# DeltaNet's inverse: the transposed copy made by transposing T, a new order of ScalarE's work between its levels, and the last heads' fillers in half units

## The chip, the cores and the metric

One core of a Trainium2 chip runs the whole program. The metric is the device time of one launch in microseconds (us), the median of the runs; a second number, the profiled execution, has its own time. TensorE is called PE in the profile, VectorE DVE, ScalarE ACT, GpSimd POOL, SyncE SP.

## The reference, cut to what matters

A trunk of two layers on 512 tokens of width 1024: gated DeltaNet, then differential attention, each followed by a gated convolutional FFN, all in float32. In DeltaNet each of 8 heads projects gate, q, k and v, convolves them over time, and solves a unit lower triangular system per chunk:

```python
low = jnp.where(strict, jnp.einsum('nbhid,nbhjd->nbhij', kb, k) * decay, 0.0)
a_mat = low + jnp.eye(C, dtype=f32)
rhs = jnp.concatenate([v * beta[..., None], kb * jnp.exp(gc)[..., None]], -1)
sol = lax.linalg.triangular_solve(a_mat, rhs, left_side=True, lower=True, unit_diagonal=True)
...
o = rms_norm(o, norm_w) * jax.nn.silu(gate.reshape(B, T, GDN_HEADS, GDN_DV))
return o.reshape(B, T, GDN_V) @ w_out
```

## The kernel before, in words

**Engines and order.** Each engine runs its own program, written out by hand in a fixed order; semaphores with counted values (`d_pe`, `d_dve`, `d_act`, `lo_ready`, `hi_ready`, ...) tie them. An instruction that waits holds all that stands behind it on its engine.

**Products in two halves.** A large product a*b is taken as three matmuls of 512 columns, a_hi*b_hi, a_hi*b_lo and a_lo*b_hi, all in fp32r. Each chunk of 128x1024 weights is loaded by SP into one of two `raw` buffers, rounded by ScalarE into `w_hi` (`split_hi`, L342), and VectorE makes the remainder `w_lo` (`split_lo`, L347); SP may load chunk c when the lo half of chunk c-2 is done, and PE may use a chunk when its lo half is done. The last four chunks of an output weight go to buffers of their own (`hold_hi`, `hold_lo`), which come free when DeltaNet's own tiles are done.

**A head's step.** While PE works head h of DeltaNet it fills the time between dependent small matmuls with pieces of the projections of head h+1: 32 pieces (`fill(p, p+1)` is one piece of three matmuls, L1533 to L1535), four chunks of eight pieces (gate, q, k, v). Small matmuls in plain float32 are two records each, transpositions one record each; `four` (L1588, or L1586 for a transposition) does all four chunks of 128 tokens.

**The inverse.** T (tile `TM`) starts as the inverse of the diagonal 8x8 blocks and doubles its blocks in four levels, s = 8, 16, 32, 64. T's transpose (`TT`) is carried beside it. One level is: P = LT*T by PE (`four`, L1588); a mask on it by VectorE into `PB` (L1084); fillers; `part(1, TT, PB, s, 0)` and `part(2, PB, TT, s, 1)` (L1595, 64 columns for each chunk of tokens), the update of T and that of TT; VectorE adds the first into `TM` (L1094, not at level 64) and the second into `TT` (L1097). Only the very first TT, before level 8, comes from a transposition, copied by ScalarE (L719). After the last level the head's V, W and the state are worked in a chain over the four chunks (L1657 to L1676), then a mean square (L1685), whose root and gate are applied by VectorE (o1, og, hi, lo; L1176 to L1182) into `u_hi`, `u_lo`.

**ScalarE between the levels:** copy of TT; silu of q and q's square for head h+1; the weight halves 8 and 9; the convolution's first tap for k; half 10.

**Last heads.** Head 7 has no next head to project: its fillers are units of the output projection (`mixer_unit(0, tb, k)`: token block tb, head k, two halves of three matmuls, L1521 to L1523), tb 0 and 1 for k = 0 to 6. They begin with a wait for both banks 0 and 1 to be read. The differences of the decay rows (L685) are the first thing that ScalarE does in a step. After the step four units of tb 2 stand before the wait for head 7's result. In attention the last head has units of its output projection as fillers in the same way, by the list `ATT_FILL`; chunks 2h+3 and 2h+4 of its q and k weights are split in step h.

Of the kernel before, what the change touches and what calls it, by code (L numbers as in the profile page):

```python
# [63 lines left out]
GDN_AHEAD = HEADS - 1  # L64
ATT_AHEAD = HEADS - 2
ATT_FILL = [(1, 0, 0), (7, 0, 1), (8, 0, 2), (9, 0, 3), (10, 1, 0), (11, 1, 1), (12, 1, 2), (13, 1, 3), (14, 0, 4),
            (14, 1, 4), (15, 0, 5), (15, 1, 5)]
# [33 lines left out]
def levels(first, then=()):  # L101
    return [f"P{LEVELS[0]}", *first, f"T{LEVELS[0]}", f"TT{LEVELS[0]}", *then] + [
        f"{k}{s}" for s in LEVELS[1:] for k in ("P", "T", "TT") if (k, s) != ("T", LEVELS[-1])]
# [3 lines left out]
PE_AT, PE_N = numbered(["kk", "qk", "kt", "lt", "bc"] + levels(["tt", "vt"])  # L107
                       + ["v0", "w", "S0", "v1", "S1", "v2", "S2", "v3", "o", "ms"])
DVE_AT, DVE_N = numbered(["L", "Lb", "Lc", "R", *SOLVE, "T0", "A", "Rw"] + levels(["kd"], ["Rv"]) + ["S0", "S1", "S2", "o1", "og", "hi", "lo"])
ACT_AT, ACT_N = numbered(["DDr", "DTr", "DD", "DT", "er", "LT", "TT", "v0", "w", "v1", "v2", "v3", "sq", "ln", "rms"])  # L110
# [25 lines left out]
def build(nc, a):  # L136
    ctx = ExitStack()
    with ctx:
# [141 lines left out]
        place_ready = sem("place_ready")  # L280
        turned = sem("turned")
# [323 lines left out]
        def _(act):  # L605
# [56 lines left out]
            def silu(h, e, r):  # L662
                dst = (qT, kT, vT)[r - 1][e]
                wait_read(act, r, 2 * h + r // 2)
                nc.scalar.activation(dst[:, :], scr[:, r % 2, :], ACT.Silu).then_inc(in_act, 1)
                if r < 3:
                    act.wait_ge(in_act, 1 + IA_N * h + IA["qk"[r - 1] + " silu"])
                    nc.scalar.activation(sq_qk[r - 1][:, :], dst[:, :], ACT.Square).then_inc(in_act, 1)


# [8 lines left out]
            def differences(h, e):  # L679
# [3 lines left out]
                for dst, col, sign, key in ((DD, neg_col, 1.0, "DDr"), (DT, gcol, -1.0, "DTr")):  # L683
# [3 lines left out]
                    ins.then_inc(d_act, 1)  # L687

            def decays(h, e):

                for dst, key in ((DD, "DDr"), (DT, "DTr")):
                    act.wait_ge(d_act, 1 + h * ACT_N + ACT_AT[key])
# [5 lines left out]
            def step(h, e, more, first=False):  # L698
# [6 lines left out]

                if not first:
                    differences(h, e)
                    decays(h, e)
# [4 lines left out]
                nc.scalar.activation(LT[e][:, :, :], v3(X(e, 0)), ACT.Copy).then_inc(d_act, 1)  # L713
# [19 lines left out]
                if more:  # L733
                    silu(h + 1, 1 - e, 2)
# [1326 lines left out]
```

## Time and profile before

| | |
|---|---|
| median of three runs | 1451.29 us (1449.49, 1451.29, 4979.85) |
| the profiled execution: time | 1453.52 us |
| its span, first to last instruction | 1451.8 us |
| granted PE clock, mean | 0.996 of 2.4 GHz |
| PE, PE weight load, DVE, ACT, POOL busy | 97%, 80%, 60%, 43%, 6% |

Between the span and the time of the same execution lie 1.7 us. DeltaNet's heads run from 61.8 us to 421.7 us of the span, 45.8 us each, attention's from 867 us to 1052 us, 21.2 us each; the rest is FFN, norms and the value projection.

### The profile page before, as it was taken

How to read it: one execution, taken by the hardware profiler on the slowest of the kernel's cores; microseconds unless marked ns; L12 is line 12 of the kernel's file. 1: busy time of each engine (PE TensorE's matmuls, PEld its weight loads, DVE VectorE, ACT ScalarE, POOL GpSimd, SP SyncE). 2: the span in 40 equal slices, each digit the busy share in tenths (PEclk: the TensorE clock that was granted, in tenths of full speed). 3: DMA queues.
4: the chain of work that ended last, by engine and by line, in shares of the span. 5: the costliest groups of instructions: out<-in, count | busy, mean ns of one | idle time of the engine just before them, and what ended most of it. 6: DMA issues, size and time to landing. Idle time of an engine off the chain costs nothing.

```text
span 1451.8 us, 20377 instructions
## 1 busy us (share of the span) xinstructions
PE 1412.9 (97%) x7138; PEld 1155.1 (80%) x7138; DVE 864.5 (60%) x1369; ACT 627.2 (43%) x1001; POOL 80.0 (6%) x92
## 2 busy tenths in 40 slices
PE   8999999999899999999999999999899999999997
PEld 7778888788779888888888776677688888888886
DVE  4665666666657666666523627777586666565226
ACT  5565455645433444444222235665524444443211
POOL 3000000000000000000000201111000000000002
PEclk9999999999999999999999999999999999999999
DMA  6212211121112333334323131122222333334231
GB/s 190 66 51 66 58 39 48 51 65 59 41 33 67 108 97 94 98 98 138 122 91 113 34 97 44 44 58 87 87 73 59 102 101 88 100 104 142 102 98 62
DMA packets 157726, 118.85 MB, mean 82 GB/s; under 512 B 5898, under 2 KB 145644, under 8 KB 157676
## 3 DMA queue, kind: packets, MB, share of 16 engines
q1 hardware_dynamic: 157676, 118.17, 27.1%
q8 instruction: 33, 0.54, 0.2%
q14 instruction: 17, 0.14, 0.0%
HBM read 116.04 MB, written 2.11 MB: 81 GB/s over the span
## 4 chain that ended last, share of the span: by engine, by line
PE 86%; DVE 8%; ACT 3%; issue 2%; DMA 1%; POOL 0%; DVEq 0%; SPq 0%; ACTq 0%
PE bank L1533 15%; PE bank L1535 15%; PE bank L1534 15%; PE bank L1521 8%; PE bank L1523 8%; PE bank L1522 8%; PE bank L1588 3%; PE bank L1595 3%; PE bank L1896 1%; PE bank L1914 1%; PE bank L1855 1%; ACT w_hi L342 1%; DVE w_lo L347 1%; DVE scr L1028 1%; PE bank L1499 1%
## 5 line engine op out<-in xcount | busy, mean ns | idle before, releaser
L1533 PE MATMUL bank<-x_hi,w_hi 128*128 128x512 f32 (+1 forms) x1160 | 457.9, 395 | 3.6 <-DVE x_lo L972 2.6
L1535 PE MATMUL bank<-x_hi,w_lo 128*128 128x512 f32 (+1 forms) x1160 | 437.5, 377 | 0.0
L1534 PE MATMUL bank<-x_lo,w_hi 128*128 128x512 f32 (+1 forms) x1160 | 436.8, 377 | 0.0
L347 DVE TENSOR_TENSOR w_lo<-raw,w_hi 128x1024 fp32r<-128x1024 f32 x194 | 237.7, 1228 | 261.1 <-ACT w_hi L342 255.7
L342 ACT ACTIVATE w_hi<-raw 128x1024 fp32r<-128x1024 f32 x186 | 194.1, 1050 | 172.4 <-PE bank L1523 139.1
L1533 PEld LDWEIGHTS bank<-x_hi,w_hi 128*128 128x128 f32 x1160 | 219.0, 189 | 43.2 <-issue 4.6
L1535 PEld LDWEIGHTS bank<-x_hi,w_lo 128*128 128x128 f32 x1160 | 218.3, 188 | 40.9
L1534 PEld LDWEIGHTS bank<-x_lo,w_hi 128*128 128x128 f32 x1160 | 219.0, 189 | 37.2 <-issue 3.3
L1521 PE MATMUL bank<-w_hi,u_hi 128*128 128x512 f32 x416 | 165.3, 397 | 4.9 <-DVE w_lo L347 2.6
L1522 PE MATMUL bank<-w_lo,u_hi 128*128 128x512 f32 x416 | 163.1, 392 | 0.0
L1523 PE MATMUL bank<-w_hi,u_lo 128*128 128x512 f32 x416 | 163.0, 392 | 0.0
L1521 PEld LDWEIGHTS bank<-w_hi,u_hi 128*128 128x128 f32 x416 | 78.9, 190 | 22.7 <-issue 3.6
L1523 PEld LDWEIGHTS bank<-w_hi,u_lo 128*128 128x128 f32 x416 | 78.8, 189 | 16.7
L1522 PEld LDWEIGHTS bank<-w_lo,u_hi 128*128 128x128 f32 x416 | 78.9, 190 | 16.5 <-issue 0.5
L855 ACT ACTIVATE u_hi<-acc_b 128x512 f32 (+1 forms) x44 | 27.8, 632 | 116.9 <-DVE acc_b L1358 116.9
L1028 DVE SCALAR_TENSOR_TENSOR scr<-bank,vec,scr 128x511 f32<-128x511 f32 (+2 forms) x72 | 53.7, 746 | 36.4 <-ACT scr L659 32.5
L852 ACT ACTIVATE acc_a<-acc_a 128x512 f32<-128x512 f32 x44 | 27.8, 632 | 78.7 <-DVE acc_a L1353 78.7
L574 POOL TENSOR_TENSOR x_tok<-x_tok,gb 128x1024 f32<-128x1024 f32 x4 | 9.6, 2397 | 824.7 <-DVE x_tok L1237 824.7
L1350 DVE SCALAR_TENSOR_TENSOR acc_b<-bank,vec,acc_b 128x511 f32<-128x511 f32 x44 | 33.0, 749 | 36.2 <-ACT acc_b L848 36.2
L1361 DVE TENSOR_TENSOR u_lo<-acc_b,u_hi 128x512 f32 (+1 forms) x44 | 30.5, 692 | 39.9 <-ACT u_hi L855 39.9
L848 ACT ACTIVATE acc_b<-bank,vec 128x512 f32<-128x512 f32 x44 | 34.2, 777 | 45.9 <-PE bank L1535 45.9
L848 ACT ACTIVATE acc_a<-bank,vec 128x512 f32<-128x512 f32 x44 | 34.2, 778 | 22.9 <-PE bank L1535 22.9
(286 smaller groups left out, 1784.6 us busy)
## 6 DMA issues: line engine op xcount, KB each, us to landing
raw<-in_ffn_w_up SPq DMA_DIRECT2D x88, 512.0 KB, 3.8
raw<-in_ffn_w_down SPq DMA_DIRECT2D x44, 512.0 KB, 3.3
raw<-in_gdn_w_in SPq DMA_DIRECT2D x32, 512.0 KB, 4.1
raw<-in_diff_w_in SPq DMA_DIRECT2D x24, 512.0 KB, 3.7
raw<-in_gdn_w_out SPq DMA_DIRECT2D x8, 512.0 KB, 3.3
raw<-in_diff_w_out SPq DMA_DIRECT2D x8, 512.0 KB, 3.2
x_tok<-in_x SPq DMA_DIRECT2D x4, 512.0 KB, 5.5
ROW<-decay_rows SPq DMA_DIRECT2D x8, 256.0 KB, 3.1
```

What stands on the lines that cost most here:

```text
L342: nc.scalar.activation(w_hi[:, s, :], raw[:, (base + r) % RAW, :], ACT.Copy).then_inc(hi_ready, 1)
L347: nc.vector.tensor_tensor(w_lo[:, s, :], raw[:, (base + r) % RAW, :], w_hi[:, s, :].bitcast(F32), ALU.subtract).then_inc(lo_ready, 1)
L848: nc.scalar.activation(acc, b[:, :], ACT.Identity, bias=fcb(l, t), scale=fcw(l, 2, t)).then_inc(f_act, 1)
L1028: ins = nc.vector.scalar_tensor_tensor(acc[:, sh:T], bank[r % 2][:, 0:T - sh], gcw(3 - sh, i * 8 + h), acc[:, sh:T], ALU.mult, ALU.add)
L1521: nc.tensor.matmul(out, hi[:, k, tok], high[:, cols], start=(k == 0), stop=False)
L1522: nc.tensor.matmul(out, hi[:, k, tok], low[:, cols], start=False, stop=False)
L1523: ins = nc.tensor.matmul(out, lo[:, k, tok], high[:, cols], start=False, stop=(k == K - 1))
L1533: nc.tensor.matmul(out, hi, x_hi[:, k, cols], start=(k == 0), stop=False)
L1534: nc.tensor.matmul(out, hi, x_lo[:, k, cols], start=False, stop=False)
L1535: ins = nc.tensor.matmul(out, lo, x_hi[:, k, cols], start=False, stop=last)
L1588: ins = nc.tensor.matmul(out, lhsT(n), rhs(n), start=True, stop=True)
L1595: ins = nc.tensor.matmul(halves(X(e, i)[:, c], s, h), lhsT[e][:, n, :], halves(rhs[e][:, n, :], s, h), start=True, stop=True)
```

## The change

**In the inverse**, part 2 is done at level 64 only. At levels 16, 32 and 64 the transposed of T is made anew: `four(2, at(TM), None, turn=True)` directly behind P, copied into TT by ScalarE. One filler then stands between these and part 1, and one behind part 1. The step has the same 32 pieces.

**ScalarE's order** between the levels becomes: copy, half 8, copy, half 9, silu of q, copy, square of q, copy, tap for k, half 10. The square of k follows silu of k as before.

**Heads 6 and 7.** The differences for head 7 move into head 6's step, ahead of the last copy. Head 6's gating (o1, og) moves into head 7's step, ahead of its first mask, and its halves (hi, lo) behind RV. VectorE's hold of chunk 4 moves ahead of KD; each of ScalarE's holds 5, 6, 7 stands ahead of one copy, and waits for head 6's halves. The fillers are half units in the list `GDN_FILL` (30, none at pieces 14 and 15), the first six of which need bank 0 or no bank of the projections; behind the step stand eight half units.

**Attention.** The splits run one chunk ahead: chunk 3 before the first step, 2h+4 and 2h+5 in step h. The last head's fillers are half units (24, as before), beginning at piece 0.

```diff
+GDN_FILL = [(0, 0, 0, 0), (1, 0, 0, 1), (2, 0, 0, 2), (3, 1, 1, 0), (4, 1, 1, 1), (5, 1, 1, 2), (6, 0, 1, 0), (7, 0, 1, 1),
+            (8, 0, 1, 2), (9, 1, 0, 0), (10, 1, 0, 1), (11, 1, 0, 2), (12, 0, 0, 3), (13, 0, 1, 3), (16, 1, 1, 3),
+            (17, 1, 0, 3), (18, 0, 0, 4), (19, 0, 1, 4), (20, 1, 0, 4), (21, 1, 1, 4), (22, 0, 0, 5), (23, 0, 1, 5),
+            (24, 1, 0, 5), (25, 1, 1, 5), (26, 2, 0, 0), (27, 2, 0, 1), (28, 2, 0, 2), (29, 0, 0, 6), (30, 0, 1, 6),
+            (31, 1, 0, 6)]
+ATT_FILL = [(0, 0, 0, 0), (1, 0, 0, 1), (2, 0, 1, 0), (3, 0, 1, 1), (5, 0, 0, 2), (6, 0, 1, 2), (7, 0, 0, 3),
+            (8, 0, 1, 3), (9, 1, 0, 0), (9, 1, 1, 0), (10, 1, 0, 1), (10, 1, 1, 1), (11, 1, 0, 2), (11, 1, 1, 2),
+            (12, 1, 0, 3), (12, 1, 1, 3), (13, 0, 0, 4), (13, 0, 1, 4), (14, 1, 0, 4), (14, 1, 1, 4), (15, 0, 0, 5),
+            (15, 0, 1, 5), (15, 1, 0, 5), (15, 1, 1, 5)]
...
@@ ScalarE, DeltaNet step
-                if not first:
+                if more and not first:
                     differences(h, e)
+                if not first:
                     decays(h, e)
...
+                if not more:
+                    hold_hi(act, C_GDN_OUT + WS, (d_dve, D_DVE0 + h * DVE_N))
...
+                def copied(s):
+                    pe(f"tt{s}")
+                    nc.scalar.activation(TT[e][:, :, :], v3(X(e, 2)), ACT.Copy).then_inc(d_act, 1)
+
                 if more:
+                    split_hi(act, C_GDN_IN, h, 8)
+                else:
+                    hold_hi(act, C_GDN_OUT + WS + 1, (o_dve, O_N * h))
+                copied(LEVELS[1])
+                if more:
+                    split_hi(act, C_GDN_IN, h, 9)
                     silu(h + 1, 1 - e, 1)
-                    split_hi(act, C_GDN_IN, h, 8)
-                    split_hi(act, C_GDN_IN, h, 9)
+                else:
+                    hold_hi(act, C_GDN_OUT + WS + 2, (o_dve, O_N * h))
+                copied(LEVELS[2])
+                if more:
+                    squared(h + 1, 1 - e, 0)
+                    if isinstance(h, int) and h == HEADS - 2:
+                        differences(h + 1, 1 - e)
+                else:
+                    hold_hi(act, C_GDN_OUT + WS + 3, (o_dve, O_N * h))
+                copied(LEVELS[3])
+                if more:
                     tap(h + 1, 2)
...
@@ VectorE, DeltaNet step
-                    pe(f"TT{s}")
+                    else:
+                        pe(f"TT{s}")
+                        act(f"TT{s}")
+                        old = halves(TT[e][:, :, :].rearrange("p n t -> p (n t)"), s, 1)
+                        nc.vector.tensor_tensor(old, halves(X(e, 2)[:, :], s, 1), old, ALU.add).then_inc(d_dve, 1)
+                if not more:
+                    gated(h - 1, 1 - e)
                 pe("kk")
...
                 masked(0)
+                if not more:
+                    hold_lo(dve, C_GDN_OUT + 4)
...
                 if not more:
-                    hold_lo(dve, C_GDN_OUT + 4)
+                    halves_out(h - 1, 1 - e)
                 masked(1)
...
+                if not (isinstance(h, int) and h == HEADS - 2):
+                    gated(h, e)
+                    halves_out(h, e)
...
@@ PE, DeltaNet step
-                    fill(p, p + 2)
-                    p += 2
-                    if i == 0:
+                        fill(p, p + 1)
+                        p += 1
                         dve("kd")
-                        act("TT")
                     else:
+                        four(2, at(TM), None, turn=True)
+                        fill(p, p + 1)
+                        p += 1
                         dve(f"P{s}")
-                        dve(f"TT{LEVELS[i - 1]}")
+                    act(f"TT{s}")
                     if s != LEVELS[-1]:
                         part(1, TT, PB, s, 0)
-                    part(2, PB, TT, s, 1)
+                        fill(p, p + 1)
+                        p += 1
+                    else:
+                        part(2, PB, TT, s, 1)
                     if more and s == LEVELS[2]:
                         square_sum(h + 1, 1 - e, 0)
+                fill(p, p + 1)
+                p += 1
                 fill(p, p + 1)
                 p += 1
                 dve(f"TT{LEVELS[-1]}")
...
-            for k in range(HELD):
-                mixer_unit(0, 2, k)
-            pe.wait_ge(d_dve, D_DVE0 + HEADS * DVE_N)
+            mixer_unit(0, 1, HEADS - 2, (1,))
+            for k in range(3):
+                mixer_unit(0, 2, k, (1,))
+            mixer_unit(0, 2, 3)
+            mixer_unit(0, 2, 4)
+            pe.wait_ge(o_dve, O_N * HEADS)
             for tb in BOTH:
                 mixer_unit(0, tb, HEADS - 1)
             mixer_rest(0)
...
@@ ScalarE and VectorE, attention (ScalarE shown; VectorE's split_lo likewise)
-                split_hi(act, C_QK, it, 2 * r + 3)
+                split_hi(act, C_QK, it, 2 * r + 4)
                 if not more:
-                    split_hi(act, C_QK, it, 2 * r + 4)
+                    split_hi(act, C_QK, it, 2 * r + 5)
...
             take(0, 1)
+            split_hi(act, C_QK, 0, 3)
             step(0, 0)
...
@@ VectorE, attention
             rope(0, 0)
+            split_lo(dve, C_QK, 0, 3)
             step(0, 0)
```

## Rows read from the trace of the kernel before

**Rows 1.** The page: busy time by engine, and the chain that ended last by engine.

```profile
PE 1412.9 (97%) x7138; PEld 1155.1 (80%) x7138; DVE 864.5 (60%) x1369; ACT 627.2 (43%) x1001; POOL 80.0 (6%) x92
...
PE 86%; DVE 8%; ACT 3%; issue 2%; DMA 1%; POOL 0%; DVEq 0%; SPq 0%; ACTq 0%
```

**Rows 2.** Busy time by stretch: span, then PE, PEld, DVE, ACT, POOL, granted clock, DMA share, GB/s.

```profile
199.13:244.89 45.76, 44.91 (x266) 37.17 (x266) 29.67 (x56) 24.92 (x44) 2.58 (x2) 1.00 0.19 52
366.43:421.68 55.25, 49.40 (x278) 40.73 (x277) 29.10 (x54) 24.52 (x41) 2.55 (x2) 0.97 0.16 48
371.00:372.00 1.00, 1.00 (x4) 0.81 (x3) 1.00 (x2) 1.00 (x4) 0.00 (x0) 0.50 0.00 0
1034.00:1035.00 1.00, 1.00 (x4) 0.81 (x3) 0.96 (x3) 1.00 (x4) 0.00 (x0) 0.50 0.62 164
```

**Rows 3.** What TensorE waited for in the whole run: us in total, times, longest.

```profile
PE bank L1521 <- DVE w_lo L347: 2.6, 1, 2.6
...
PE bank L1521 <- DVE scr L1028: 2.3, 1, 2.3
...
PE bank L1521 <- DVE gdn_lo L360: 1.3, 1, 1.3
```

**Rows 4.** PE in order of time, head 3: start, duration, instruction.

```profile
200.12 0.60 PE L1586 MATMUL bank<-ident,TM 128*128 128x128 f32 x4
200.48 0.47 PE L1533 MATMUL bank<-x_hi,w_hi 128*128 128x512 f32 x1
...
203.07 1.00 PE L1595 MATMUL bank<-PB,TT 128*128 128x64 f32 x8
203.91 1.06 PE L1595 MATMUL bank<-TT,PB 128*128 128x64 f32 x8
204.80 1.11 PE L1588 MATMUL bank<-TM,LT 128*128 128x128 f32 x8
205.67 0.48 PE L1533 MATMUL bank<-x_hi,w_hi 128*128 128x512 f32 x1
...
206.45 0.39 PE L1533 MATMUL bank<-x_hi,w_hi 128*128 128x512 f32 x1
...
212.91 1.08 PE L1551 MATMUL bank<-sq_q,ones 128*128 128x512 f32 x2
214.06 1.16 PE L1588 MATMUL bank<-TM,LT 128*128 128x128 f32 x8
```

**Rows 5.** ScalarE in order of time, the same head.

```profile
200.76 0.60 ACT L719 ACTIVATE TT<-bank 128x512 f32<-128x512 f32 x1 [0.86 <-PE bank L1586]
...
211.37 1.99 ACT L342 ACTIVATE w_hi<-raw 128x1024 fp32r<-128x1024 f32 x2
```

**Rows 6.** VectorE in order of time, the same head.

```profile
201.53 1.22 DVE L347 TENSOR_TENSOR w_lo<-raw,w_hi 128x1024 fp32r<-128x1024 f32 x1
...
205.95 0.69 DVE L1084 TENSOR_TENSOR PB<-bank,level 128x512 f32<-128x512 f32 x1
...
213.59 0.42 DVE L1094 TENSOR_TENSOR TM<-bank,TM 128x256 f32<-128x256 f32 x1
```

**Rows 7.** The page's DMA issues: KB each, median us from issue to landing.

```profile
raw<-in_gdn_w_in SPq DMA_DIRECT2D x32, 512.0 KB, 4.1
```

**Rows 8.** PE in order of time, the last DeltaNet head and what follows it.

```profile
366.43 1.12 PE L1685 MATMUL bank<-PB,mean_h 128*128 128x512 f32 x2
369.87 0.47 PE L1521 MATMUL bank<-w_hi,u_hi 128*128 128x512 f32 x1 [2.32 <-DVE scr L1028]
...
421.68 0.50 PE L1521 MATMUL bank<-gdn_hi,u_hi 128*128 128x512 f32 x1
```

**Rows 9.** PE and VectorE in order of time, attention's first and last head.

```profile
871.05 0.49 PE L1896 MATMUL bank<-kr,qr 64*128 64x128 f32 x4
...
1026.37 2.35 DVE L347 TENSOR_TENSOR w_lo<-raw,w_hi 128x1024 fp32r<-128x1024 f32 x2
...
1033.32 0.79 PE L1521 MATMUL bank<-w_hi,u_hi 128*128 128x512 f32 x1 [2.62 <-DVE w_lo L347]
```

More of the change, by code:

```diff
@@ L769, in _ @@
             step(0, 0, True, first=True)
-            with act.Fori(0, PAIRS - 1) as it:
+            with act.Fori(0, PAIRS - 2) as it:
                 for e in (1, 0):
                     step(2 * it + 2 - e, e, True)
+            step(HEADS - 3, 1, True)
+            step(HEADS - 2, 0, True)
             step(HEADS - 1, 1, False)
@@ L1094, in added @@
                         nc.vector.tensor_tensor(old, halves(X(e, 1)[:, :], s, 0), old, ALU.add).then_inc(d_dve, 1)
-                    pe(f"TT{s}")
-                    old = halves(TT[e][:, :, :].rearrange("p n t -> p (n t)"), s, 1)
-                    nc.vector.tensor_tensor(old, halves(X(e, 2)[:, :], s, 1), old, ALU.add).then_inc(d_dve, 1)
+                    else:
[5 more added lines that the diff above has]
+                    gated(h - 1, 1 - e)
                 pe("kk")
@@ L1513, in tile, with unit @@
                     block_products(t % 2, s, k, k == KT - 1)
-            def unit(i, tb, k, c, K, hi, lo, held, done):
+            def unit(i, tb, k, c, K, hi, lo, held, done, which=BOTH):
                 pe.wait_ge(lo_ready, c + 1)
                 tok, (high, low) = slice(tb * P, (tb + 1) * P), chunk_at(c)
-                for half in range(2):
+                for half in which:
                     out, cols = bank[OUT_BANKS[i][tb][half]][:, :], slice(half * T, (half + 1) * T)
@@ L1551, in square_sum, with mixer_unit @@
                 nc.tensor.matmul(X(e, i)[:, :], ones[:, :], sq_qk[i][:, :], start=True, stop=True).then_inc(in_sums, 1)
[L1553 to L1554 removed]
+            def mixer_unit(l, tb, k, which=BOTH):
+                unit(2 * l, tb, k, (C_GDN_OUT, C_ATT_OUT)[l] + k, HEADS, u_hi, u_lo, tb == NT - 1, k == HEADS - 1, which)
             def step(h, e, more):
@@ L1806, in mixer_rest @@
             def mixer_rest(l):
-                for k in range(HELD, HEADS):
+                for k in range(HELD + 1 - l, HEADS):
                     mixer_unit(l, 2, k)
@@ L1878, in fill @@
                     if last:
-                        for q in range(len(ATT_FILL)):
-                            if p0 <= ATT_FILL[q][0] < p1:
-                                if q == 0:
-                                    pe.wait_ge(bank_read[0], T_UP[1] // 2 + 1)
-                                    pe.wait_ge(bank_read[1], T_UP[1] // 2 + 1)
-                                if ATT_FILL[q][1:] == (1, 0):
-                                    act("exp", 2, 1)
-                                mixer_unit(1, *ATT_FILL[q][1:])
+                        for tb, half, k in [piece for p, *piece in ATT_FILL if p0 <= p < p1]:
+                            if (tb, k) == (0, 0):
+                                pe.wait_ge(bank_read[half], T_UP[1] // 2 + 1)
+                            if (tb, half, k) == (1, 0, 0):
+                                act("exp", 2, 1)
+                            mixer_unit(1, tb, k, (half,))
                     else:
```

99 lines of the change are left out of this document (50 added, 49 removed).

## The prediction

> **What bounds the kernel now.** First the page: PE is busy 97% of the span and holds 86% of the chain that ended last [rows 1]. So time goes only if PE gets less work or stands idle for less. Then the busy time by stretch, one head of DeltaNet beside the last one: a middle head takes 45.76 us with 44.91 us of PE busy, while the last head, to the wait for its result, takes 55.25 us with 49.40 busy and a mean clock of 0.97 [rows 2]. Then the list of PE's waits: the longest that the change touches are one each of 2.6, 2.3 and 1.3 us [rows 3]. After the first two the granted clock was 0.50 of 2.4 GHz, which is 1.2 GHz [rows 2]: a stretch of about 3.4 us each time, by its means 3.4 x 0.5 = 1.7 us lost. After the wait of 1.3 us it stayed at 2.4 GHz: 1.7 us of 55.25 is 0.03, the whole of what that stretch's mean lacks. Last the three engines in order of time within one head, which gives the duration and cover of each step.
>
> **The change, part by part.** I lay the new order out by hand over head 3's rows, from start to start, since matmuls overlap.
>
> *PE's work in the inverse.* Part 2 costs 204.80 - 203.91 = 0.89 us, four transpositions 200.48 - 200.12 = 0.36 us [rows 4]. Three of part 2 go (levels 8, 16, 32), three sets of transpositions come (16, 32, 64): 3 x (0.89 - 0.36) = 1.60 us less. A filler behind float32 work takes 206.45 - 205.67 = 0.78 us, one behind another filler 0.69, estimated from its three products at 0.23 [rows 4]. The split fillers make three more such starts: 3 x 0.09 = 0.27 us more. VectorE loses three sums of 0.42, ScalarE gains three copies of 0.60 [rows 5, 6]; both have room (29.7 and 24.9 us of 45.8 busy [rows 2]), so only their latency counts.
>
> *The new wait, part 1 for TT.* The copy starts 200.76 - 200.12 = 0.64 us after the transpositions and takes 0.60 [rows 4, 5]; with 0.05 us for the signal (the sum of T32 ended at 214.01, P64 began at 214.06 [rows 4, 6]) TT is there 1.29 us after the transpositions began. Part 1 could begin after 0.36 + 0.78 = 1.14. That is 0.15 idle, and the first small matmul after a wait is about 0.12 longer (P's 1.11 against 1.16, and a lost early weight load): 0.27 us, at three levels 0.81. Behind the waiting part 1 stand a filler and the next P. The bounds are 0, if PE hides it, and 0.6 a level, if the copy is late by another such instruction. I take 0.27. The mask comes no later: P's product ends 1.11 after its start, then 0.04 + 0.69 + 0.05, against 0.87 + 0.36 + 0.78 = 2.01 us to part 1 [rows 4, 6]. The sum of T after part 1 takes 1.00 + 0.04 + 0.42 + 0.05 = 1.51 us, its cover 0.83 + 0.78 = 1.61 with one filler only [rows 4, 6]: it just holds, at 0.02.
>
> *ScalarE's order.* Before, half 8 was made at 211.37, behind silu of q; VectorE waited for it and reached T32's sum at 213.59, so P64 began at 214.06 [rows 4 to 6]. The float32 square sum before P64 began at 212.91 and takes 0.86, so P64 could have begun at 213.77: 0.29 us of wait, which goes, with 0.04 of restart. Is a copy now late behind a half? Half 8 starts right after the first copy, near 201.3, and is done at 202.4, three us before the second. Half 9 stands ahead of silu of q and the third copy. Its load is released by half 7's lo, 201.53 + 1.22 = 202.75 [rows 6], and takes 4.1 us at the page's median [rows 7]: 206.9, done at 207.9, silu by 208.9. The third copy is due at 209.27. Slack 0.4 to 1.3 us. Square of q (0.63) lies in front of nothing but the next copy, 3.9 us later.
>
> *One head.* Saved 1.60 + 0.33, spent 0.27 + 0.81 + 0.03: 0.82 us. From V on, the order is the old one with its waits. Seven heads: 5.7 us. Bounds per head: 0.3 (copies late by more) and 1.6 (no exposure): 2 to 11 us.
>
> *Head 7.* Before, PE ended head 6's mean square at 366.43 + 0.86 and waited until 369.87 for VectorE's taps, since the fillers asked for both banks; then the clock fell for 3.4 us [rows 2, 3, 8]. Now six half units, 6 x 0.69 = 4.1 us, need neither: the wait goes (2.3 us by its row) and with it the clock's 1.7. What is late next: with less filler before it, the solve on VectorE (the 8x8 blocks) ends at about 381.8 while PE has run out at 380.2, as pieces 14 and 15 are empty: 1.6 us idle. Then hold_lo of chunk 4 ahead of KD costs PE 0.5, and the copy of T16 stands on ScalarE behind hold_hi of chunk 5, which waits for head 6's halves, now made by VectorE after RV: those end at about 388.75, the hold at 389.8, the copy at 390.4, PE stands 1.3. The old waits for chunk 4's lo (1.3 [rows 3]), for the mask at level 64 and for W go or shrink, being covered by single halves. Laid out so to the end, head 7's result is there at 417.5 instead of 421.68 [rows 8], 4.2 us earlier. PE has by then done 38 half units, before 36 (28 + 8 against 30 + 8), so 2 x 0.69 = 1.4 us of work is also behind it: 5.5 us. The norm's chain that follows on VectorE moves with it. Bounds 3.5 (the clock falls in the new idle of 1.6, which lies between the 1.3 that left it and the 2.3 that didn't) and 6.5.
>
> *Attention, first head.* VectorE makes chunk 3's lo, 1.2 us [rows 6], ahead of the rotation of k, for which the scores at 871.05 wait [rows 9]: they begin at about 872.15, 1.1 us later, and nothing in that step takes it back. Other steps split at the same places a chunk ahead: nothing.
>
> *Attention, last head.* Before, PE idled 2.6 us until 1033.32 for w_lo, which waited for its load, and the clock fell [rows 2, 3, 9]. Chunks 18 and 19 are now loaded a step ahead, so that wait goes. But the list puts (0, 0, 2) at piece 5, ahead of the second turn, and that unit needs chunk 18's lo, which VectorE makes only after the third maxima, from 1026.5 to 1027.7 (its place in [rows 9]). PE is there at 1024.6: 3.2 us of new wait, behind which stand the turn, the last scores and ScalarE's exponentials. Afterwards two units more than before are done, and PE runs through. By the layout the step ends 3.4 us earlier with the clock kept, 1.7 with its fall; as both waits above 2 us were followed by one, I take 1.7. Bounds 0.5 and 3.4.
>
> *Sum.* 5.7 + 5.5 - 1.1 + 1.7 = 11.8 us. The profiled execution took 1453.52 us (span 1451.8 + 1.7 around it); it would take 1441.7. The median shown is 2.2 us lower: 1451.29 - 11.8 = 1439.5 us, 0.8% less.
>
> **A page that speaks against it.** Four transpositions take 0.36 us here, 90 ns each [rows 4]. The Trainium skill (TensorE: Matmul & The Clock Gate, Part 4: PE-mode transpose) gives about 275 ns for one in a kernel, and says that they don't count as activity for the clock. By its figure a set would take 1.1 us, and the inverse would lose 0.6 us a head instead of winning 1.6 before the waits; the trace disagrees on the duration.
>
> **Rivals.**
> *A, late load (slower than before).* Half 9 waits on ScalarE for its load ahead of silu and the third copy. From a landing at 207.6 on, 4.9 us after issue, each further us is a us of PE idle in each of seven heads. From 6.6 us after issue the whole gain is eaten; at 8 us it costs 3.2 x 7 = 22: 1462 us. For it: one queue carries all loads. Against it: 4.1 us at the median and a DMA share of 0.19 in that stretch [rows 2, 7]. 4%.
> *B, no exposure.* The next weight load and the filler's tail hide the 0.27 us of each copy: 0.81 x 7 = 5.7 us more, 1434 us. For it: PE loads weights early; against it: the same signal path cost P64 its full wait [rows 4, 6]. 12%.
> *C, the last heads pay more.* The new idle stretches in head 7 also bring the clock down, 1.7 us, and its waits add up to 2 more: 1443 us. For it: 1.6 and 1.3 us of idle there lie close together. 18%.
> *D, the inverse gives nothing.* What is saved between P8 and V returns as a wait before the next P8, because the chain of taps, norms, gating and solve on VectorE binds. For it: that chain already ends late by 0.2 us in each head. Against: it begins at the head's end and so moves with it. 1439.5 + 5.7 = 1445 us. 8%.
> *E, the clock falls in each head.* If the transpositions left PE too little active, one fall a head, 7 x 1.7 = 12 us, would give 1451 us. For it: nothing here but the three small idles near them. Against: a middle head already has four sets and waits of 0.3, at clock 1.00 [rows 2]. 2%. The skill's sentence above on the clock would be its reason.
>
> **How the numbers follow.** The forecast has 56%, A 4, B 12, C 18, D 8, E 2. Unknown costs make its own range 1436 to 1443. For 8 times in 10 it must reach C and D and the near side of B: 1434.5 to 1446. A difference under 2% is about what a measurement of this kernel can't tell from no change; 2% is 29 us, faster than 1422 or slower than 1480. No case but an extreme A reaches either: faster 0.01, within 0.98, slower 0.01.
>
> **What would show it.** In a middle head the way from P8 to V's first product is 18.1 us instead of 18.9, the head 44.9 instead of 45.8; L1595 has 32 records a head, not 56, and part 1 at levels 16, 32 and 64's part 2 wait 0.1 to 0.2 us for ScalarE's copy; VectorE no longer waits 1.7 us for half 8. No wait of 2.3 us at head 7's start and no clock of 0.5 there, but about 1.6 us before its P8 and 1.3 before part 1 at level 16. Attention's first scores come 1.1 us later in their step, and its last head waits about 3 us for chunk 18's lo at half unit (0, 0, 2). I am wrong if the copies are seldom on time, if a copy waits behind half 9, or if the chain before P8 stretches.

## The result, and the profile after

The changed kernel takes **1442.4 us** (median of 5 executions, 1440.9 to 1443.8) against 1451.3: the ratio is 0.9935, 95% interval 0.992 to 0.995, or 7 to 12 us less. A second set of executions gave 1442.9 and 0.9936 (0.9922 to 0.9950). The forecast was 1439.5 with a range of 1434.5 to 1446. The profiled execution took 1441.09 us (1453.52 before), where the prediction's sum had 1441.7. The two comparisons, 12.4 us between profiled executions and about 9 between medians, are taken up below. P8, P16, P32 and P64 stand for the product P of a level, V and W for the two products that follow the last level.

**The page** of the changed kernel, busy time and chain, as in [rows 1]:

```profile
PE 1401.9 (97%) x7042; PEld 1138.1 (79%) x7042; DVE 858.0 (60%) x1345; ACT 640.7 (45%) x1025; POOL 80.2 (6%) x92
...
PE 88%; DVE 8%; ACT 2%; issue 1%; DMA 1%; POOL 0%; SPq 0%; DVEq 0%; ACTq 0%
```

PE is busy for 11.0 us less and the span is 12.5 us shorter. The instruction count confirms the edit: 96 matmul records less, which is 8 heads x 3 levels x (8 - 4).

**Busy time by stretch**, as in [rows 2]: head 3 from P8 to P8, head 7 from head 6's mean square to its own result, and two single microseconds for the clock.

```profile
195.45:240.35 44.90, 44.15 (x254) 35.58 (x254) 28.73 (x53) 26.61 (x47) 2.58 (x2) 1.00 0.20 53
359.46:410.67 51.21, 47.71 (x272) 38.44 (x271) 28.66 (x51) 23.97 (x36) 2.57 (x2) 1.00 0.17 52
371.00:372.00 1.00, 1.00 (x6) 0.81 (x5) 0.89 (x4) 0.00 (x1) 0.00 (x0) 1.00 0.00 0
1018.00:1019.00 1.00, 1.00 (x4) 0.80 (x3) 0.23 (x1) 0.00 (x0) 0.00 (x0) 0.50 0.89 197
```

A middle head is 0.86 us shorter, head 7 4.04. The clock no longer falls in head 7, and still falls in attention's last head.

**What PE waited for**, as in [rows 3]: us in total, times, longest.

```profile
PE bank L1571 <- DVE w_lo L357: 3.0, 1, 3.0
...
PE bank L1639 <- DVE TM L1172: 1.8, 2, 1.6
...
PE bank L1954 <- DVE kr L1436: 1.7, 1, 1.7
...
PE bank L1646 <- ACT TT L735: 1.1, 1, 1.1
```

The three waits of before are gone. In their place stand four: for chunk 18's lo (3.0), before P8 of head 7 (1.6), before attention's first scores (1.7) and for a copy of TT in head 7 (1.1).

**PE in head 3**, as in [rows 4]: L1639 makes P, L1637 the transpositions, L1646 part 1 (at level 64 part 2), L1601 the square sum, L1714 V.

```profile
195.45 1.16 PE L1639 MATMUL bank<-TM,LT 128*128 128x128 f32 x8
...
201.23 0.60 PE L1637 MATMUL bank<-ident,TM 128*128 128x128 f32 x4
...
202.51 1.10 PE L1646 MATMUL bank<-PB,TT 128*128 128x64 f32 x8
...
208.11 1.02 PE L1601 MATMUL bank<-sq_q,ones 128*128 128x512 f32 x2
...
208.97 1.05 PE L1639 MATMUL bank<-TM,LT 128*128 128x128 f32 x8
...
211.15 1.10 PE L1646 MATMUL bank<-TT,PB 128*128 128x64 f32 x8
...
213.53 0.38 PE L1714 MATMUL bank<-RV,TT 128*128 128x128 f32 x2
```

From P8 to V it is 213.53 - 195.45 = 18.08 us. Part 1 at level 16 begins 1.28 us after its transpositions. P64 follows the square sum after 0.86 us, its plain duration: its old wait is gone.

**ScalarE in the same head**, as in [rows 5]: the copies (L735), half 9 (L352) and silu of q (L674) with what ended the idle time before each.

```profile
201.86 0.60 ACT L735 ACTIVATE TT<-bank 128x512 f32<-128x512 f32 x1 [3.23 <-PE bank L1637]
203.26 1.06 ACT L352 ACTIVATE w_hi<-raw 128x1024 fp32r<-128x1024 f32 x1 [0.80 <-DMA raw<-in_gdn_w_in]
204.77 0.63 ACT L674 ACTIVATE qT<-scr 128x512 f32<-128x512 f32 x1 [0.45 <-DVE scr L1062]
205.77 0.60 ACT L735 ACTIVATE TT<-bank 128x512 f32<-128x512 f32 x1 [0.37 <-PE bank L1637]
```

The copy at level 16 ends at 202.46 and part 1 starts 0.05 later. Half 9 waited 0.80 us for its load, and the next copy still started in time.

**PE in head 7**, as in [rows 8]: P8, part 1 at level 8 and 16, and the first use of the head's result.

```profile
374.89 1.13 PE L1639 MATMUL bank<-TM,LT 128*128 128x128 f32 x8 [1.56 <-DVE TM L1172]
...
378.54 1.10 PE L1646 MATMUL bank<-PB,TT 128*128 128x64 f32 x8 [0.25 <-DVE KD L1184]
...
383.54 1.08 PE L1646 MATMUL bank<-PB,TT 128*128 128x64 f32 x8 [1.08 <-ACT TT L735]
...
410.67 0.50 PE L1571 MATMUL bank<-gdn_hi,u_hi 128*128 128x512 f32 x1
```

**Attention**, PE and VectorE together, as in [rows 9]: chunk 3's lo half and the first scores of the first step, then the half unit (0, 0, 2) in the last.

```profile
857.54 1.63 DVE L357 TENSOR_TENSOR w_lo<-raw,w_hi 128x1024 fp32r<-128x1024 f32 x1
...
860.55 0.49 PE L1954 MATMUL bank<-kr,qr 64*128 64x128 f32 x4 [1.70 <-DVE kr L1436]
...
1017.15 0.50 PE L1571 MATMUL bank<-w_hi,u_hi 128*128 128x512 f32 x1 [3.02 <-DVE w_lo L357]
```

**Where the 12.5 us of span went.** Laid side by side from landmark to landmark: the seven steps of heads 0 to 6 give 6.1 us (0.86 in the first, 0.87 as the mean of the six others). Head 7 gives 4.04, and two half units more done ahead of its result, 1.4. Attention's first step costs 1.56: from its first rotation to its scores 854.90 to 860.55 now, 866.96 to 871.05 before. Its last step, from rotation to the turning of its result, gives 2.02. That is 12.0 us; the 1.4 is the prediction's two half units at 0.69, not a stretch read by itself. The other 0.5 is not the change's: the first P8 came 0.9 us earlier (60.88 against 61.76), most of it since x was read sooner in this execution (first projection at 11.40 against 12.17), and 0.35 was lost between the layers. There PE waits for the normed x between the first FFN and attention, 1.59 us against 1.22 before, which accounts for it.

### The profile page after: what moved, and what is told of

Same layout as the page of the kernel before. It is cut to its first block, busy times and chain, and to the rows that moved or that the text cites. A ratio compares the mean times of both kernels' runs of the same rounds, so it can differ in the third digit from the quotient of the medians.

```text
span 1439.3 us, 20095 instructions
## 1 busy us (share of the span) xinstructions
PE 1401.9 (97%) x7042; PEld 1138.1 (79%) x7042; DVE 858.0 (60%) x1345; ACT 640.7 (45%) x1025; POOL 80.2 (6%) x92
## 4 chain that ended last, share of the span: by engine, by line
PE 88%; DVE 8%; ACT 2%; issue 1%; DMA 1%; POOL 0%; SPq 0%; DVEq 0%; ACTq 0%
PE bank L1583 16%; PE bank L1585 16%; PE bank L1584 16%; PE bank L1571 8%; PE bank L1573 8%; PE bank L1572 8%; PE bank L1639 3%; PE bank L1646 2%; PE bank L1954 2%; PE bank L1972 1%; PE bank L1637 1%; PE bank L1915 1%; PE bank L1601 1%; DVE w_lo L357 1%; PE bank L1717 1%
## 5 line engine op out<-in xcount | busy, mean ns | idle before, releaser
L352 ACT ACTIVATE w_hi<-raw 128x1024 fp32r<-128x1024 f32 x186 | 195.0, 1051 | 168.0 <-PE bank L1573 139.8
L1572 PEld LDWEIGHTS bank<-w_lo,u_hi 128*128 128x128 f32 x416 | 78.3, 188 | 16.3 <-issue 0.5
```

Of the source, the lines that this page charges most:

```text
L352: nc.scalar.activation(w_hi[:, s, :], raw[:, (base + r) % RAW, :], ACT.Copy).then_inc(hi_ready, 1)
L1572: nc.tensor.matmul(out, hi[:, k, tok], low[:, cols], start=False, stop=False)
```

## The experiments

All are edits of the changed kernel, and all times are beside new executions of the kernel before, which took 1449.5 to 1455.0 us. A head's length is given from mean square to mean square.

### The inverse undone

```diff
 # PE, levels 16 to 64
-                        four(2, at(TM), None, turn=True)
-                        fill(p, p + 1)
-                        p += 1
+                        fill(p, p + 2)
+                        p += 2
                         dve(f"P{s}")
+                        dve(f"TT{LEVELS[i - 1]}")
...
                     if s != LEVELS[-1]:
                         part(1, TT, PB, s, 0)
-                        fill(p, p + 1)
-                        p += 1
-                    else:
-                        part(2, PB, TT, s, 1)
+                    part(2, PB, TT, s, 1)
 # ScalarE: silu of q and its square first, no copies
+                    silu(h + 1, 1 - e, 1)
+                    squared(h + 1, 1 - e, 0)
                     split_hi(act, C_GDN_IN, h, 8)
-                copied(LEVELS[1])
```

> The changed kernel with the old inverse and ScalarE's old order between its levels; the lists of half units, head 6's gating in head 7's step and attention's splits stay changed. The prediction's own theory: each middle head goes from 44.9 to 45.7 us and the way from P8 to V's first product from 18.1 to 18.9, so the whole is 5.7 us slower than the changed kernel, near 1448 us. Rival D (the inverse gives nothing, the chain before P8 binds): the way from P8 to V is 18.9, but the head stays at 44.9 and the time at 1442.

Measured 1447.9 us (9 executions, ratio 0.9969, 0.9959 to 0.9979): 5.0 to 5.5 us above the changed kernel. The heads take 45.75 us instead of 44.87, and the way from P8 to W 19.17 instead of 18.30. All of what is saved before V is saved in the head too, so rival D falls. One thing was not foreseen: head 7 takes 44.37 us with the old inverse and 44.56 with the new one. There the new inverse gains nothing. PE waits 1.08 us for a copy that stands behind one of ScalarE's holds and 0.25 for KD, where with the old inverse it waits 0.5 for a mask. But the holds ahead of the copies are not the whole cause: with them moved (below) another wait takes the place of the first.

### ScalarE's order alone

```diff
 # on top of the last
-                    silu(h + 1, 1 - e, 1)
-                    squared(h + 1, 1 - e, 0)
                     split_hi(act, C_GDN_IN, h, 8)
                     split_hi(act, C_GDN_IN, h, 9)
+                    silu(h + 1, 1 - e, 1)
+                    squared(h + 1, 1 - e, 0)
```

> The run with the old inverse, but with ScalarE's half 8 and half 9 ahead of silu of q and its square: the order alone. The prediction's term: VectorE no longer waits for half 8, P64 comes without its wait, 0.33 us a head, so the heads take 45.4 instead of 45.75 us. Rival: in the old inverse half 9's load holds silu of q back, and the square sum is late instead, so that the heads stay at 45.75 or more.

One execution, 1447.2 us. The window from P8 to P8 of a middle head, with the old order and with the new one:

```profile
152.72:198.47 45.75, 44.89 (x267) 37.19 (x267) 29.48 (x56) 24.95 (x44) 2.57 (x2) 1.00 0.19 52
```

```profile
153.40:198.78 45.38, 44.60 (x266) 37.27 (x266) 29.65 (x56) 25.04 (x44) 2.59 (x2) 1.00 0.21 52
```

Over heads 1 to 6 the mean is 45.41 us, 0.34 less than 45.75. So of the 0.88 us a head 0.34 is the order and 0.54 the transpositions; the prediction had 0.33 and 0.49. The way from P8 to W says the same: 19.17, 18.83 and 18.30 us.

### Each copy in two instructions

```diff
-                    nc.scalar.activation(TT[e][:, :, :], v3(X(e, 2)), ACT.Copy).then_inc(d_act, 1)
+                    for n in (slice(0, 2), slice(2, 4)):
+                        nc.scalar.activation(TT[e][:, n, :], v3(X(e, 2))[:, n, :], ACT.Copy).then_inc(d_act, 1)
 # PE, part(): wait for the first instruction before chunk 0, for the second before chunk 2
+                        if s != LEVELS[0] and n in (0, 2):
+                            act(f"{'TT' if n or s == LEVELS[-1] else 'TU'}{s}")
```

> The changed kernel with each of ScalarE's copies of the transposed T (levels 16, 32, 64) in two instructions of 256 columns; part 1 waits for the first, and for the second only before its third chunk (part 2 at level 64 waits for both). Theory (part 1 stands idle for the copy): the first half is there 0.2 us earlier, so part 1 starts without the idle of 0.15 at levels 16 and 32, and the way from P8 to V's first product shrinks from 18.08 to between 17.5 and 17.8, a head from 44.9 to between 44.4 and 44.7, 2 to 4 us in all. Rival (the restart or the mask on VectorE binds as well): nothing is gained, 18.1 and 44.9.

Measured 1440.9 us (median of 4 executions from 1437.9 to 1444.4; ratio 0.9914, 0.9893 to 0.9935), 1.5 to 2.1 us below the changed kernel. The profiled execution is the longest of the four, with three falls of the clock after DeltaNet, so the gain is read from its heads, where the clock is 1.00. PE in head 3, transpositions and part 1 at level 16:

```profile
202.38 0.60 PE L1638 MATMUL bank<-ident,TM 128*128 128x128 f32 x4
...
203.51 1.04 PE L1649 MATMUL bank<-PB,TT 128*128 128x64 f32 x8
```

Part 1 now begins 1.13 us after the transpositions, where [rows 4] gave 1.14 for no wait, and the heads take 44.52 us, 0.35 less, which is near 2.5 us over seven heads. So part 1 does stand idle for the copy, and the wait can be taken away at levels 16 and 32. At level 64, where part 2 writes the bank that the second instruction reads, it stays.

### Half 9 ahead of the second copy

```diff
                     split_hi(act, C_GDN_IN, h, 8)
+                    split_hi(act, C_GDN_IN, h, 9)
...
                 copied(LEVELS[1])
                 if more:
-                    split_hi(act, C_GDN_IN, h, 9)
                     silu(h + 1, 1 - e, 1)
```

> The changed kernel with ScalarE's weight half 9 ahead of the copy of T16 instead of behind it: rival A, a late load in front of a copy, made to happen. Half 9's load lands near 203.2 us in head 3, so the half ends at 204.1 and the copy at 204.7, and part 1 at level 16 begins at 204.75 instead of 202.51: 2.2 us in each of seven heads, 15.7 in all, 1458 us, slower than the kernel before. If PE's queue hid such a delay, or the later waits of the head took it back (the rival), the time would stay within 3 us of 1442.

One execution, 1472.0 us: 30 above the changed kernel, twice the expected price. The wait itself came as expected:

```profile
219.12 1.10 PE L1646 MATMUL bank<-PB,TT 128*128 128x64 f32 x8 [2.38 <-ACT TT L735]
```

Two neighbouring heads of the same execution, by window:

```profile
178.33:225.59 47.26, 44.09 (x256) 35.60 (x255) 28.70 (x53) 26.51 (x47) 2.57 (x2) 1.00 0.18 50
225.59:275.75 50.16, 47.00 (x256) 38.59 (x254) 28.78 (x53) 26.52 (x47) 2.58 (x2) 0.93 0.19 51
```

The first is 44.87 + 2.38 us long, with the clock at 1.00. In the second the clock fell after the same wait, for 6.8 us, and it is 2.9 longer. In all, six of seven such waits were followed by a fall, three of 3.4 us and three of 6.8: 15.4 us by the mean clock, and about 13 by the lengths of the heads (1.4 and 2.9 us each). The waits for copies themselves are 17.4 us in eight heads by the list of PE's waits, 1.1 in the changed kernel. So 16.3 us of waits and about 13 of falls make the 30. Rival A's mechanism is real, and dearer than the prediction had it.

### Both banks again at head 7's start

```diff
-                            if (tb, k) == (0, 0):
-                                pe.wait_ge(bank_read[half], T_UP[0] // 2 + 1)
+                            if (tb, half, k) == (0, 0, 0):
+                                pe.wait_ge(bank_read[0], T_UP[0] // 2 + 1)
+                                pe.wait_ge(bank_read[1], T_UP[0] // 2 + 1)
```

> The changed kernel, where the first half unit of head 7 waits for both banks again. Theory: it waits 2.3 us for VectorE's taps, the granted clock falls to 0.50 for about 3.4 us after it, and head 7's result comes 2.3 + 1.7 - 0.3 = 3.7 us later than in the changed kernel. Rival 1: the wait comes back but no clock falls, 2.0 to 2.3 us later. Rival 2: kk waits for the norm of k anyway, so that nothing is lost: 0.

Median 1446.1 us (6 executions from 1443.7 to 1448.4; ratio 0.9962, 0.9949 to 0.9974), 3.2 to 3.7 above the changed kernel. The profiled execution is the fastest of the six. The wait is back in it:

```profile
362.96 0.47 PE L1571 MATMUL bank<-w_hi,u_hi 128*128 128x512 f32 x1 [2.22 <-DVE scr L1062]
```

But the clock held, as the window after it shows, and head 7 was 47.03 us long instead of 44.56, so 2.5 lost:

```profile
363.00:366.00 3.00, 3.00 (x13) 2.48 (x14) 2.52 (x4) 3.00 (x8) 0.00 (x0) 1.00 0.00 0
```

So the wait is worth 2.5 us at once. The fall that followed it in the kernel before doesn't come each time. The median's further 0.7 to 1.2 us would fit such falls in some of the executions; that is not shown, as the others have no profile.

### Attention's half units behind the turn

```diff
-ATT_FILL = [..., (5, 0, 0, 2), (6, 0, 1, 2), (7, 0, 0, 3), ...]
+ATT_FILL = [..., (7, 0, 0, 2), (7, 0, 1, 2), (7, 0, 0, 3), ...]
```

> The changed kernel with the half units (0, 0, 2) and (0, 1, 2) of attention's last head at piece 7, behind the turn and scores of block 1 and 3, instead of pieces 5 and 6. Theory: of the 3.0 us of wait for chunk 18's lo about 1.0 stays, for the turn's input (ready at 1015.0), the clock keeps 2.4 GHz, and the step ends 2.0 + 1.7 = 3.7 us earlier: 1438.7 us. Rival 1: the clock falls even so, 2.0 us. Rival 2: the wait only moves to the scores or the values behind it: 0.

Measured 1439.4 us (ratio 0.9915, 0.9898 to 0.9931). PE before the second turn of the last step, and the window after it:

```profile
1016.39 0.44 PE L1966 MATMUL bank<-ident,Pm 128*128 128x128 f32 x2 [0.95 <-DVE Pm L1489]
```

```profile
1017.00:1021.00 4.00, 4.00 (x21) 2.76 (x20) 3.96 (x7) 1.46 (x6) 0.00 (x0) 1.00 0.42 137
```

The step from rotation to the turning of its result takes 29.36 us instead of 32.95, 3.6 less. The wait of 3.0 and the fall were thus the price of the place on the list, as the prediction said, and nothing behind them took it back: the 0.95 us before the turn stand in the kernel before too (0.96).

### Chunk 3's lo half inside attention's first step

```diff
-            split_lo(dve, C_QK, 0, 3)
             step(0, 0)
 # VectorE, attention step
                 maxima(1)
+                if first:
+                    split_lo(dve, C_QK, 0, 3)
```

> The changed kernel, in which VectorE makes chunk 3's lo half inside attention's first step, behind the second maxima, instead of ahead of the rotation of k. Theory: the first scores come 4.1 us after the first rotation, as in the kernel before, instead of 5.65, and nothing behind takes it back: 1.6 us less. Rival 1: the lo half then delays the mixing on VectorE and the turn of block 2 waits 1 us more, leaving 0.5. Rival 2: it is late for the projection of the next head: a wait of over 1 us at piece 8.

Measured 1440.4 us (ratio 0.9919, 0.9900 to 0.9937). The first scores come 4.10 us after the first rotation (855.06 to 859.16), 1.55 less, and the wait of 1.7 us is gone. The only wait behind, 0.53 us for the turn of block 2, is the one that the changed kernel has too.

### Head 7: the holds behind the copies, then packed

```diff
 # holds_behind, ScalarE, head 7: chunks 5, 6, 7 each one copy later
-                    hold_hi(act, C_GDN_OUT + WS + 1, (o_dve, O_N * h))
                 copied(LEVELS[1])
+                    hold_hi(act, C_GDN_OUT + WS + 1, (o_dve, O_N * h))
 # head7_packed, in addition
-            ... (16, 1, 1, 3), (17, 1, 0, 3), ...
+            ... (14, 1, 1, 3), (15, 1, 0, 3), ...
                 masked(0)
-                if not more:
-                    hold_lo(dve, C_GDN_OUT + 4)
                 nc.vector.tensor_tensor(KD[e][:, :, :], v3(X(e, 2)), bc(kdecs), ALU.mult).then_inc(d_dve, 1)
+                if not more:
+                    hold_lo(dve, C_GDN_OUT + 4)
```

> The changed kernel with ScalarE's holds of chunks 5, 6 and 7 each one copy later in head 7. Theory: the wait of 1.08 us before part 1 at level 16 goes, as the copy no longer stands behind a hold that waits for head 6's halves, and head 7's result comes 1.1 us earlier. Rival: the mask at level 16, which VectorE makes behind the same halves at 382.3 us, is late next, and only 0.2 us are won: or a hold that is later starves a half unit, and nothing is.

One execution, 1440.9 us. PE with the holds behind, part 1 at level 16 and P64:

```profile
382.64 1.07 PE L1646 MATMUL bank<-PB,TT 128*128 128x64 f32 x8
...
389.05 1.16 PE L1639 MATMUL bank<-TM,LT 128*128 128x128 f32 x8 [0.62 <-DVE TM L1147]
```

The wait of 1.08 us goes, but the head is only 0.16 us shorter. A later one has come, 0.62 us before P64, and the expectation was wrong. It is a wait for the sum of T at level 32, ahead of which VectorE has its hold of chunk 6, and that now waits for ScalarE's; the rows of the next run show it.

> Holds behind the copies as in the run before, and in addition the half units of pieces 16 and 17 at pieces 14 and 15, where TensorE stood idle for the solve, and VectorE's hold of chunk 4 behind KD again. Theory: P8 begins at the same distance from head 7's start (the solve on VectorE sets it), but part 1 at level 8 follows it after 2.5 us instead of 3.65, and the level 16 after that waits only for the mask: head 7 is 2.0 to 2.5 us shorter than in the changed kernel. Rival: head 7 is bound by the latency from P8 on, so that the missing fillers turn up as waits at other levels and less than 1 us is won.

Median 1441.6 us (ratio 0.9928, 0.9909 to 0.9947), which doesn't tell it from the changed kernel; its windows do. PE in head 7:

```profile
375.35 1.13 PE L1639 MATMUL bank<-TM,LT 128*128 128x128 f32 x8 [0.22 <-DVE TM L1172]
...
377.86 1.10 PE L1646 MATMUL bank<-PB,TT 128*128 128x64 f32 x8 [0.51 <-DVE KD L1182]
```

P8 keeps its distance from the head's start (15.48 us, 15.43 before the edit) and part 1 follows after 2.51 instead of 3.65, both as expected. The head is 1.04 us shorter and not 2.0 to 2.5. The 0.62 before P64 is there again, which is one part of the reason; that the levels behind run at PE's pace with their fillers is the likely rest, not shown by itself. VectorE shows the wait that holds the sum at level 32:

```profile
386.86 1.23 DVE L370 TENSOR_TENSOR gdn_lo<-raw,gdn_hi 128x1024 fp32r<-128x1024 f32 x1 [1.32 <-ACT gdn_hi L365]
388.00 0.42 DVE L1147 TENSOR_TENSOR TM<-bank,TM 128x256 f32<-128x256 f32 x1
```

### All together

Copies in two, attention's half units behind the turn, chunk 3's lo half in the step, head 7 packed, and VectorE's hold of chunk 6 behind the sum:

```diff
-                    hold_lo(dve, C_GDN_OUT + 6)
                 added(2)
+                if not more:
+                    hold_lo(dve, C_GDN_OUT + 6)
```

> All of what helped, in one kernel: copies in two, attention's half units at piece 7, chunk 3's lo half inside attention's first step, head 7 packed, and VectorE's hold of chunk 6 behind the sum of T at level 32, since that hold, waiting for ScalarE's hold of chunk 6, held the sum and cost TensorE 0.6 us before P64. Theory: 2.5 (copies) + 3.6 (half units) + 1.55 (chunk 3) + 1.0 + 0.6 (head 7) = 9.3 us less than the changed kernel: near 1433 us, some 18 to 19 less than the kernel before. Rival: the parts overlap (a later wait takes the place of one removed), which leaves 6 us or less: 1436 or more.

**1432.95 us**, ratio 0.9867 (0.9851 to 0.9884) to the kernel before: 17 to 22 us less than it, and 9.4 to 10.0 below the two medians of the changed kernel. A middle head from P8 to P8, and head 7 from mean square to mean square:

```profile
105.36:149.95 44.59, 43.77 (x255) 35.60 (x255) 28.79 (x53) 26.78 (x50) 2.59 (x2) 1.00 0.21 54
357.10:399.37 42.27, 40.99 (x246) 33.93 (x245) 26.12 (x47) 18.69 (x34) 2.56 (x2) 1.00 0.21 63
```

Head 7 is 2.29 us shorter than in the changed kernel, and the 0.6 before P64 is gone from PE's waits; the parts add up in the medians (9.3 expected), and the rival of overlap falls. The profiled execution is only 8.1 us below that of the changed kernel (1441.09). It has a fall of its own, with a wait of 2.39 us between the layers, where the changed kernel waits 1.59:

```profile
787.07 1.33 PE L1551 MATMUL bank<-ident,x_tok 128*128 128x128 f32 x5 [2.39 <-POOL x_tok L586]
```

### The changed kernel once more

> The changed kernel once more, unedited, against more executions of the kernel before. Why were the medians 8.9 us apart and the profiled executions 12.4? Theory: falls of the clock after the same wait come in some executions and not in others, each 1.7 us, so a kernel's executions spread by about 4 us at granted clocks of 0.996 to 0.998, and the gap lies between 9 and 12 us: ratio 0.992 to 0.994. Rival: the change is worth only what the medians first showed, 9 us or less, and the one profiled execution of before was slow by chance elsewhere: ratio 0.994 or more.

1442.9 us (6 executions, 1441.5 to 1445.9), ratio 0.9936 (0.9922 to 0.9950): at the lower end of the theory's gap, not clear of the rival's edge. What the profile of this execution shows is one fall more than the first had, after the same wait of 1.7 us for attention's first scores:

```profile
863.00:864.00 1.00, 1.00 (x7) 0.55 (x4) 0.45 (x2) 0.48 (x4) 0.00 (x0) 0.50 0.57 170
```

It lasted 3.4 us. By its mean clock that is 1.7 us. With a first projection 0.8 us later, 12.16 against 11.40, it makes the 2.4 us between two executions of one kernel.

## Why the prediction was right, and where it was off

**A middle head, -0.82 us: -0.88.** Right in each step. P8 to V is 18.08 us (18.1 said). Part 1 begins 0.15 us after PE could have, the copy and its 0.05 us of signal as laid out, and the run with copies in two shows that this idle was real. The order is worth 0.34 (0.33 said), shown by itself. The transpositions are worth 0.54 (0.49 said), as a set of four takes 0.35 us of PE from its start to the next instruction's. The sum of T after part 1 was covered, as laid out: no wait stands before P16 or P32 in head 3. Its slack was 1.61 - 1.51 = 0.10 us by the prediction's own terms, not the 0.02 that it gives. Rival B (no exposure) is refuted, rival D too. E is as well: the clock is 1.00 in every middle head. Rival A didn't happen, since half 9's load came 0.80 us after ScalarE asked for it. The run that puts it ahead of the copy shows that its price would have been paid in full.

**The paragraph "A page that speaks against it"** misreads its figure. The records of the kernel before, in head 3:

```profile
L1586 PE MATMUL bank<-ident,TM x4: 273/273/273, 200.1 to 200.4; 128*128 128x128 f32 x4
```

Each transposition is 273 ns long by its record, whose end is modelled, so the trace doesn't disagree on the duration with the 275 ns that the prediction takes from the Trainium skill (TensorE: Matmul & The Clock Gate, Part 4: PE-mode transpose). The four overlap: their starts are 0.11 us apart, and PE's next instruction starts 0.36 us after the first. The duration times four, 1.1 us, was never the price of a set; the prediction's sum was right to go from start to start.

**Head 7, -5.5 us: -5.4** (4.04 and 1.4) in the profiled executions. The three new waits are there with the sizes that the layout gave, 1.56 (1.6), 0.25 (0.5) and 1.08 (1.3), and rival C's fall in them never came. What the prediction didn't see is that the inverse gives nothing in this head. The other error is that it booked the clock's 1.7 us as certain. The same wait, put back, left the clock alone in its profiled execution. Of the 5.4 only the 2.5 of that wait is shown by an experiment. The fall beside it is read from the trace of before, and no run undoes the moved gating, the holds or attention's earlier splits by themselves.

**Attention's first step, +1.1 us: +1.56.** The mechanism was right, the term of the lo half too small: it took 1.63 us and not 1.2. It ran beside an instruction of GpSimd, told below.

**Attention's last step, -1.7 us: -2.0.** The new wait was 3.0 us (3.2 said), and the clock fell, as the prediction chose between its two bounds. Every profile that has this wait has the fall, ten of ten, and in two of them it lasted twice as long.

**The sum, -11.8 us: -12.0** of profiled time, and the profiled execution was hit to 0.6 us. A part of that is luck: the terms are off by up to 0.5 us each, in both directions, and the second profiled execution of the same kernel took 1443.41 us. **The median is 2.9 us above the forecast.** The step that was off is the last one: "The median shown is 2.2 us lower: 1451.29 - 11.8 = 1439.5 us". It took the whole difference of one pair of executions over to the medians. But the execution profiled before was one of the longer ones, with both falls in it. Others ran from 1449.5 to 1455.0 us at mean clocks of 0.995 to 0.998. In the changed kernel one chance of a fall has gone (head 7) and another has come: after the new wait of 1.7 us for the first scores the clock fell in five of ten profiles. By that count the new wait costs 0.8 us more on average (an estimate, half of 1.7), and the old one in head 7 was worth less than its 1.7 if its like in the run with both banks is a guide. That accounts for a part of the 2.6 us between the traces' 12.0 and the 9.4 of the ratios; the rest lies inside the interval, 7 to 12 us, and stays open, as executions without a profile show their mean clock only.

## What to carry to other kernels

A product that only keeps a transposed copy up to date can be dropped for a transposition where another engine has room for the copy; cost it by the start-to-start times of PE, and count the restart of the matmul that waits, then halve the wait by copying in two instructions. When a wait is taken away, lay out by hand what is late next on each engine's queue: three of the four new waits here came from a filler, a lo half or a hold that stood a little too early, and moving these (3.6, 1.55 and about 2 us) was worth more than the 6.1 of the inverse and its order. And a loss by a clock fall seen in one execution is an estimate with odds, not a term: compare profiled executions only after counting the falls in both.

## What the runs showed of the hardware that was not expected

**A fall of the clock with idle time is not determined by the length of the wait alone.** Over the thirteen profiles here, as the granted clock shows from DeltaNet's first head on:

| PE's wait | times seen | 1.2 GHz came with it or after it |
|---|---|---|
| 3.0 us, chunk 18's lo | 10 | 10 |
| 2.6 us, w_lo in the kernel before | 1 | 1 |
| 2.4 and 2.7 us, the normed x between the layers (all together, copies in two) | 2 | 2 |
| 2.2 to 2.6 us, late copies (half 9 first) | 7 | 6 |
| 2.3 and 2.2 us, VectorE's taps (before, both banks) | 2 | 1 |
| 1.7 us, attention's first scores | 10 | 5 |
| 1.2 to 1.7 us, the normed x in the other profiles | 11 | 0 |
| 1.6 us, head 7's P8 | 10 | 0 |

No other fall stands between the first head and the last few microseconds of a run. Two waits at the same place of two heads in the run with half 9 first, one of 2.38 us without a fall and one of 2.20 us with one, show that the length doesn't decide alone. The fall began before the wait had ended in several profiles, 1.8 us before at most. Why the wait between the layers is 2.4 and 2.7 us in the two profiles with copies in two and at most 1.7 in all others isn't shown. A fall lasted 3.4 us or 6.8 us, nothing between, and made a head of the run with half 9 first 1.4 or 2.9 us longer (48.69 and 50.15 beside 47.26 without a fall, from W to W).

**GpSimd stretches some of VectorE's instructions.** Chunk 3's lo half started at 857.54 us while a copy ran on GpSimd, and it took 1.63 us. Two others of the same kind did so, beside products on GpSimd:

```profile
50.07 1.28 POOL L572 TENSOR_TENSOR QD<-qT,ER 128x512 f32<-128x512 f32 x1 [33.29 <-ACT ER L704]
50.80 1.63 DVE L357 TENSOR_TENSOR w_lo<-raw,w_hi 128x1024 fp32r<-128x1024 f32 x1 [2.10 <-ACT w_hi L352]
...
850.54 1.29 POOL L596 TENSOR_TENSOR rope<-qk_raw,cos 128x512 f32<-128x512 f32 x1 [54.22 <-ACT qk_raw L916]
851.29 1.62 DVE L357 TENSOR_TENSOR w_lo<-raw,w_hi 128x1024 fp32r<-128x1024 f32 x1 [15.58 <-ACT w_hi L352]
...
857.02 1.07 POOL L601 COPY vh<-v_tok 128x512 f32<-128x512 f32 x1
```

Of 194 such instructions these three are the longest by far. The median is 1.225 us, and all that ran with GpSimd idle took 1.21 to 1.23. Each of the three began 0.54 to 0.55 us before GpSimd's instruction ended and took 0.40 us longer than the median, and the other profiles show such pairs too, with 1.62 to 1.64 us each. Beside the masks that GpSimd builds in the program's first 15 us the same instruction took at most 1.30 us. In the run where the rotation of k stands at the place of chunk 3's lo half, VectorE's product with a bank as one operand took 0.68 us beside the same copy, which is its usual time. The Trainium skill (SBUF — State Buffer, SBUF: two separate sides) says that a VectorE instruction with two inputs in SBUF and a GpSimd instruction that reads SBUF exclude each other, the later one standing still until the other ends. The trace agrees in the main: who is stretched and who isn't is as it says, but the stretch is 0.40 us where standing still for the whole overlap would make 0.55, and the masks, some of which are read from SBUF too, hardly stretched anything.
